# Two-layer decoder trunk on one core: the last head's searches, four tiles, one unit's gate and the summed blocks of stick-breaking attention are put elsewhere

## The chip, the cores and the metric

One core of a Trainium2 chip runs the whole kernel in one launch. The metric is the device time of an execution in microseconds. A core has TensorE (PE, matrix products into PSUM), VectorE (DVE), ScalarE (ACT), GpSimd (POOL, which here masks weights and issues the indirect row fetches) and SyncE (SP, which issues the other transfers). Each engine works through its own list of instructions in order, and they wait for one another by counting semaphores.

## The reference

512 tokens of 1024 float32 values pass two layers. A layer has a token mixer and a channel mixer, each behind an RMSNorm with shift and gain from a conditioning vector.

The token mixer has eight stick-breaking heads and four differential heads. For a stick-breaking head

```
log_fail = where(key < query, log_sigmoid(-z), 0)
after    = sum of log_fail over later keys
w        = where(key < query, exp(log_sigmoid(z) + after), 0);   y = w @ v
```

The channel mixer retrieves single-neuron experts. Each of eight heads scores a token against two sets of 128 keys, takes the best 16 of each (s, i), then the best 16 of the 256 sums, which name 16 of 16384 experts, with a softmax over their sums as gates g:

```
a = h . u[expert];  y = sum over 8 heads x 16 picks of  gelu(a) * g * v[expert]
```

## The kernel before

**Token mixer.** Four turns a layer, each with two stick-breaking heads (h = 0, 1) and one differential head. The keys are taken in four blocks of 128 from the last to the first: block p has kb = 3 - p, and its scores are kept for the queries from 128 kb on, 512 - 128 kb columns. `logits` makes z, ScalarE's `soften` the softplus, and VectorE (L1263, L1267) stores L = softplus, masked on the diagonal. `sums(p)` adds to z in PSUM the products NEG_UPPER @ L[kb] (L660) and NEG_ONES @ L[kk] for every later block kk (L663): none at p=0, 128 columns at p=1, 256 and 128 at p=2, and 384, 256 and 128 at p=3. Then ScalarE (`weigh`) exponentiates, GpSimd masks, and `values` multiplies with v. A float32 product is two instructions in the trace. Beside this VectorE makes the modulation of the next stage (L1207) and the rotary rope of dq (after block 2) and dk (after block 3).

**Channel mixer.** Tokens 0 to 255 (two chunks) take their experts by rows: 16 units (chunk x head), each 16 rows of u and 16 rows of v, 512 rows a layer, numbered in one sequence. GpSimd fetches row n with an indirect DMA (L1166) into a ring of eight as soon as row n - 8 is used; VectorE takes the product with a u row (L1417) or adds a v row (L1423). Ahead of a unit's v rows stand `gate_rows`, which needs ScalarE's exponential and gelu of that unit (`unit_gates`), and `topk` of the unit two further on, so at row 160 that of unit 6 and at row 192 that of unit 7.

Tokens 256 to 511 go densely, against all 16384 experts: 128 tiles of 128, in two halves of 64. TensorE transposes a tile of u (`turn_u`, L548, one tile ahead), ScalarE copies it out (L978), TensorE multiplies it with h (L558), and ScalarE applies gelu to a pair (L911). This starts beside the eight heads' queries (L525) and scores (L535): eight tiles stand behind each of heads 0 to 5, none behind head 6, and sixteen behind head 7. The query weights of a head are loaded by SyncE as soon as the scores before have read the buffer.

VectorE finds the dense tokens' picks meanwhile (`topk_dense`, one for each head and chunk, ending in L1379), ten rows between one search and the next. For each pair of heads ScalarE exponentiates (`gates_t`, L923) and VectorE divides (`gates_dense`, L1386 to L1390); that of the last pair stands on ScalarE ahead of tile 60 and signals `pre_done`. TensorE then transposes the picks (`turn_picks`), ScalarE copies them out (`picks_out`), and the map stage makes the gate of every expert for every dense token, in 32 batches of 8 tokens: VectorE's `columns` (L1432, L1437) and ScalarE's `p_batch` (L946, L950) make one-hot columns, TensorE multiplies them (L589), VectorE's `gate_batch` (L1448) multiplies the activations by the gates, and ScalarE's `keep_batch` (L962) keeps the second half's gates. VectorE takes one row after each batch, 164 to 195. In batch 16 ScalarE does `unit_gates(5)`.

Then come, on TensorE, the value tiles of the first half (L605), the activation tiles of the second half, and its value tiles. VectorE goes on with the rows from 196; with rows 368 and 432 start 32 kept gate products each (L1465), the first of which waits for the second half's activations. At the layer's end x is loaded back and both sums are added (L1504 to L1514).

The order on every engine is written out by hand; nothing plans it.

Of the kernel before, what the change touches and what calls it, by code (L numbers as in the profile page):

```python
# [66 lines left out]
G_BANK = [6, 4]  # L67
KEPT = 4
KEEP0 = 16 * 23
KEEP1 = 16 * 27  # L70
# [42 lines left out]
def build(nc, io, out):  # L113
    with ExitStack() as ctx:
# [93 lines left out]
        def small(*dims):  # L208
# [38 lines left out]
            "q_ev k_ev v_ev dqraw_ev dkraw_ev dv_mm dv_ev rope_mm dq_ready dk_ready "  # L247
            "z_done  ln_done L_done b_done w_exp w_masked pv_done ysb_ev "
            "s_done max_done p_exp dw_done wt_done wt_ev y_done y_sq yn_done yt_done yd_ev "
# [19 lines left out]
        def qcols(kb):  # L269
            return SEQ - P * kb  # L270
# [5 lines left out]
        def _(sp):  # L276
# [35 lines left out]
            with sp.Fori(0, DEPTH) as l:  # L312
# [114 lines left out]
                spill_x(CH - 1)  # L427
                for hd in range(HEADS - 2):
                    load_q(hd + 1)
                    more_u(8 * hd + 4, 8)  # L430
                load_q(HEADS - 1)
                more_u(HALF - 12, 12)
                all_v(0)
# [21 lines left out]
        def _(pe):  # L455
# [167 lines left out]
            def mix(i, last_turn):  # L623
# [31 lines left out]
                def sums(p):  # L655
                    kb = CH - 1 - p
                    for h in range(2):
                        bank = 2 + 2 * (p % 2) + h
                        pe.wait_ge(S["L_done"], 8 * i + 2 * p + h + 1)
                        last = pe.matmul(ps[:, bank, 0:qcols(kb)], C(NEG_UPPER), L[:, h, kb, 0:qcols(kb)],  # L660
                                         start=False, stop=(kb == CH - 1), skip_group_check=True)
                        for kk in range(kb + 1, CH):
                            last = pe.matmul(ps[:, bank, (kk - kb) * P:qcols(kb)], C(NEG_ONES),  # L663
                                             L[:, h, kk, 0:qcols(kk)], start=False, stop=(kk == CH - 1),
                                             skip_group_check=True)
                        last.then_inc(S["b_done"], 1)
# [99 lines left out]
            with pe.Fori(0, DEPTH) as l:  # L766
# [41 lines left out]
                for hd in range(HEADS):  # L808
                    query(l, hd, 0)
                    query(l, hd, 1)  # L810
                    head_scores(l, hd)
                    if hd == 0:
                        turn_u(l, 0, 0)
                    if hd < HEADS - 2:
                        act_tiles(l, 0, 8 * hd, 8 * hd + 8)
                act_tiles(l, 0, 8 * (HEADS - 2), HALF)
                turn_picks(l)
# [8 lines left out]
        def _(act):  # L826
# [160 lines left out]
            def channel_mix(l):  # L987

                for hd in range(HEADS):
                    stage_query(l, hd, 0)  # L990
                    stage_query(l, hd, 1)
                    stage_scores(l, hd)
                    if hd == 0:
                        u_out(l, 0, 0)
                    if hd % 2 == 0 and hd > 0:
                        gates_t(l, hd // 2 - 1)
                    if hd in (1, 2, 4, 5, 7):
                        unit_gates(l, (1, 2, 4, 5, 7).index(hd))
                    if hd < HEADS - 2:
                        for tile in range(8 * hd, 8 * hd + 8):  # L1000
                            act_tile(l, 0, tile)
                for tile in range(8 * (HEADS - 2), HALF):
                    if tile == HALF - 4:
                        gates_t(l, BLOCKS - 1)
                    act_tile(l, 0, tile)
                picks_out(l)
                for b in range(NB):
                    p_batch(l, b)
                    if b >= 1:
                        keep_batch(l, b - 1)  # L1010
                    if b == 16:
                        unit_gates(l, 5)
                keep_batch(l, NB - 1)
                for j in range(6, 9):
                    unit_gates(l, j)
# [164 lines left out]
        def _(dve):  # L1180
# [70 lines left out]
            def mix(i, t):  # L1251
# [6 lines left out]
                for p in range(CH):  # L1258
# [7 lines left out]
                    for h in range(2):  # L1266
                        dve.tensor_tensor(L[:, h, kb, 0:P], L[:, h, kb, 0:P], C(STRICT), ALU.mult).then_inc(S["L_done"], 1)  # L1267
                    dve.drain()
                    if p == 2:
                        rope(i, 0, dq_raw, dq, 0, "dq_ready")  # L1270
# [178 lines left out]

            def gate_maps(l, row0):  # L1450

                for b in range(NB):
                    columns(l, b)
                    if b >= 1:
                        gate_batch(l, b - 1)
                    rows(l, row0 + b, row0 + b + 1)
                gate_batch(l, NB - 1)
# [17 lines left out]
            def channel_mix(l):  # L1475

                dve.wait_ge(S["tr_done"], 4 * CH * l + 4 * CH)
                park()
                for hd in range(HEADS):
                    rows(l, 20 * hd, 20 * hd + 10)  # L1480
# [5 lines left out]
                    if hd % 2 == 0 and hd > 0:  # L1486
                        gates_dense(l, hd // 2 - 1)
                gates_dense(l, BLOCKS - 1).then_inc(S["pre_done"], 1)
                rows(l, 160, 164)
                dve.wait_ge(S["pq_ev"], ND * l + ND)  # L1490
                park()
                gate_maps(l, 164)
                rows(l, 196, KEEP0)
                kept_maps(l, 0, KEEP0)
# [164 lines left out]
```

## Time and profile before

| | us |
|---|---|
| median of 3 runs | 3883.69 (3882.17 to 3885.43) |
| profiled execution, its own time | 3883.39 |
| its span, first to last instruction | 3881.7 |
| TensorE busy | 3505.5 (90%) |
| VectorE busy | 2624.1 (68%) |
| GpSimd busy | 1382.6 (36%) |
| ScalarE busy | 981.8 (25%) |

All times in rows are microseconds from the span's start, if not marked ns. The chain that ended last is 61% TensorE and 24% VectorE; the rest is issue, transfers and ScalarE.

### The profile page before, as it was taken

What the parts mean: (1) busy time and instruction counts of PE and PEld (TensorE: products, weight loads), DVE (VectorE), ACT (ScalarE), POOL (GpSimd) and SP (SyncE); (2) the same over time, 40 slices, a digit from 0 to 9 for tenths busy, and PEclk for the clock granted to TensorE, in tenths of its full rate; (3) what the DMA queues carried; (4) which work ended last, traced back from release to release, by engine and by line L of the source; (5) the groups of instructions that cost most, each with busy time, mean ns of one, the idle gap of its engine ahead of it and who ended that gap; (6) DMA issues with size and microseconds to landing.
All of it is one profiled execution on the core that took longest, in us unless ns stands there. A gap on an engine that the chain in (4) does not pass through costs nothing.

```text
span 3881.7 us, 50533 instructions
## 1 busy us (share of the span) xinstructions
PE 3505.5 (90%) x13822; PEld 2245.4 (58%) x13822; DVE 2624.1 (68%) x5585; ACT 981.8 (25%) x2147; POOL 1382.6 (36%) x1220
## 2 busy tenths in 40 slices
PE   4998998999866999999978889989998579999997
PEld 2555444777654448884445554457767544688643
DVE  6555115899899777777555541279999987777774
ACT  1333102323254003330023330123223620133200
POOL 0000001445423665566500000034444245666663
PEclk9999999999988999999989999999998889999999
DMA  6321224788856999999952222168877579999997
GB/s 243 132 103 55 91 83 169 283 314 322 303 171 220 404 394 396 337 386 384 374 198 103 97 82 103 50 251 328 307 273 283 179 295 399 401 381 334 391 390 297
DMA packets 274015, 999.71 MB, mean 258 GB/s; under 512 B 31353, under 2 KB 48249, under 8 KB 262785
## 3 DMA queue, kind: packets, MB, share of 16 engines
q0 software_dynamic: 153600, 553.72, 37.7%
q1 hardware_dynamic: 120194, 443.42, 30.3%
q8 instruction: 92, 1.51, 0.2%
q14 instruction: 129, 1.06, 0.1%
HBM read 971.85 MB, written 25.17 MB: 257 GB/s over the span
## 4 chain that ended last, share of the span: by engine, by line
PE 61%; DVE 24%; issue 5%; DVEq 5%; DMA 3%; ACT 2%; ACTq 0%; POOL 0%; SPq 0%; POOLq 0%
PE ps L605 22%; PE ps L558 12%; PE ps L784 9%; DVE arena L1417 4%; DVE mod L1423 4%; PE ps L548 3%; DVE arena L1207 3%; PE ps L516 2%; DMA arena<-in_u_dram,idx 2%; PE ps L493 2%; PE ps L613 2%; PE ps L637 1%; DVE mod L1437 1%; DVEq L1425 1%; DVE arena L1313 1%
## 5 line engine op out<-in xcount | busy, mean ns | idle before, releaser
L1166 POOL DMA_INDIRECT arena<-in_u_dram,idx x512 | 647.5, 1265 | 1001.4 <-issue 648.4
L558 PE MATMUL ps<-hT,mod 128*128 128x256 f32 x4096 | 927.8, 380 | 0.0
L605 PE MATMUL ps<-arena 128*128 128x512 f32 x2048 | 881.6, 593 | 3.7 <-ACT hT L962 3.7
L1166 POOL DMA_INDIRECT arena<-in_v_dram,idx x512 | 638.8, 1248 | 621.8 <-DVE mod L1423 369.5
L558 PEld LDWEIGHTS ps<-hT,mod 128*128 128x128 f32 x4096 | 760.2, 191 | 93.3
L1417 DVE CUSTOM_DVE_ANT_0 arena<-arena 128x1024 f32<-128x1024 f32 x512 | 616.6, 1223 | 236.7 <-DMA arena<-in_u_dram,idx 233.1
L1423 DVE SCALAR_TENSOR_TENSOR mod<-arena,mod 128x1024 f32<-128x1024 f32 x512 | 657.1, 1283 | 122.7 <-DMA arena<-in_v_dram,idx 93.5
L605 PEld LDWEIGHTS ps<-arena 128*128 128x128 f32 x2048 | 389.6, 190 | 493.3 <-issue 493.2
L978 ACT COPY mod<-ps 128x512 f32<-128x512 f32 x512 | 274.6, 590 | 553.1 <-PE ps L548 553.1
L548 PE MATMUL ps<-const,arena 128*128 128x128 f32 x2048 | 269.0, 275 | 20.1 <-ACT mod L978 19.2
L548 PEld LDWEIGHTS ps<-const,arena 128*128 128x128 f32 x2048 | 239.1, 141 | 51.1 <-ACT mod L978 26.6
L525 PE MATMUL ps<-hT,arena 128*128 128x512 f32 x512 | 230.7, 610 | 14.0 <-DMA arena<-in_w_q_dram 11.7
L1207 DVE SCALAR_TENSOR_TENSOR arena<-arena,c_act 128x256 f32<-128x256 f32 x448 | 213.7, 484 | 40.9 <-DMA arena<-in_ada_w_dram 9.2
L1145 POOL TENSOR_SCALAR_AFFINE_SELECT arena<-arena 128x128 f32<-128x128 f32 x32 | 11.7, 378 | 615.8 <-ACT arena L1051 615.8
L784 PE MATMUL ps<-hT,arena 128*128 128x512 f32 x512 | 228.3, 605 | 2.7 <-ACT arena L1095 2.7
L1549 DVE TENSOR_TENSOR arena<-arena,ps 128x512 f32<-128x512 f32 x32 | 22.0, 688 | 306.6 <-PE ps L784 306.6
L525 PEld LDWEIGHTS ps<-hT,arena 128*128 128x128 f32 x512 | 99.9, 196 | 135.6 <-issue 135.0
L784 PEld LDWEIGHTS ps<-hT,arena 128*128 128x128 f32 x512 | 99.3, 194 | 128.2 <-issue 128.2
L911 ACT ACTIVATE arena<-ps 128x512 f32<-128x512 f32 x128 | 76.9, 601 | 371.6 <-PE ps L558 371.6
L589 PE MATMUL ps<-arena,mod 128*128 128x128 f32 x512 | 84.9, 334 | 76.9 <-issue 39.4
L589 PE MATMUL ps<-cos_sin,mod 128*128 128x128 f32 x512 | 86.5, 339 | 56.7 <-ACT mod L950 38.9
L516 PE MATMUL ps<-hT,arena 128*128 128x512 f32 x288 | 132.2, 614 | 3.2 <-ACT hT L860 1.9
(201 smaller groups left out, 3493.1 us busy)
## 6 DMA issues: line engine op xcount, KB each, us to landing
arena<-in_u_dram SPq DMA_DIRECT2D x256, 512.0 KB, 7.1
arena<-in_v_dram SPq DMA_DIRECT2D x256, 512.0 KB, 6.8
arena<-in_ada_w_dram SPq DMA_DIRECT2D x56, 1024.0 KB, 5.7
arena<-in_w_qkv_dram SPq DMA_DIRECT2D x48, 512.0 KB, 6.3
arena<-in_w_m_dram SPq DMA_DIRECT2D x16, 1536.0 KB, 6.8
arena<-in_w_q_dram SPq DMA_DIRECT2D x32, 576.0 KB, 6.5
gate_scratch<-hT SPq DMA_DIRECT2D x64, 256.0 KB, 2.2
hT<-gate_scratch POOLq DMA_DIRECT2D x128, 128.0 KB, 7.8
```

The source lines that it names most:

```text
L516: last = pe.matmul(ps[:, bank, :], w_qkv[:, g, k, :], hT[:, k, :], start=(k == 0), stop=(k == KD - 1))
L525: last = pe.matmul(ps[:, c, :], q_w[:, c, k, :], hT[:, k, :], start=(k == 0), stop=(k == KD - 1))
L548: last = pe.transpose(ps[:, 4 + h, k * P:(k + 1) * P], stream[:, slot, kk * P:(kk + 1) * P], C(IDENT))
L558: last = pe.matmul(ps[:, 6 + tile // 2 % 2, tile % 2 * NT:(tile % 2 + 1) * NT], u_turned[:, tile % 2, k * P:(k + 1) * P], hT[:, k, DT0:SEQ ...
L589: last = pe.matmul(ps[:, G_BANK[s] + t // 4, t % 4 * P:(t % 4 + 1) * P], p1[:, s, t * P:(t + 1) * P], q1[s][:, t * P:(t + 1) * P], start=T ...
L605: last = pe.matmul(ps[:, 2 * c + n, :], act_t[:, e, c * P:(c + 1) * P], stream[:, slot, n * 512:(n + 1) * 512], start=(half == 0 and e == ...
L784: last = pe.matmul(ps[:, 4 * s + b, :], w_m[:, s, k0 + k, :], rhs[:, k, :], start=(k == 0), stop=(k == n - 1))
L978: act.copy(u_turned[:, tile % 2, h * 512:(h + 1) * 512], ps[:, 4 + h, :]).then_inc(S["ut_ev"], 1)
L1166: pool.indirect_dma_start(out=ring[:, r % RING, :], out_offset=None, in_=table, in_offset=bass.IndirectOffsetOnAxis(ap=idx[:, j % 4, k:k + ...
L1207: last = dve.scalar_tensor_tensor(acc, ada_w[at % 3][:, k, :], c_act[:, k:k + 1], bias[:, cols] if k == 0 else acc, ALU.mult, ALU.add)
L1417: dve.tensor_tensor_reduce(row, row, h2[:, j % 2, :], 1.0, 0.0, ALU.mult, ALU.add, dots[:, j % 2, k:k + 1]).then_inc(S["row_used"], 1)
L1423: dve.scalar_tensor_tensor(total, row, coef[:, k:k + 1], total, ALU.mult, ALU.add).then_inc(S["row_used"], 1)
```

## The change

In the map stage and around it:

- Tiles 44 to 47 stand behind head 6's scores and no longer ahead of its query. SyncE's loads follow: head 7's query weights are issued ahead of tile 48's transfer.
- On VectorE head 7's two searches and the last `gates_dense` stand ahead of rows 140 to 159. Rows 140 to 160 stand between it and the maps; the maps take rows 161 to 191, and the last batch takes none.
- On ScalarE the last `gates_t` stands behind tile 63, ahead of `picks_out`, and `unit_gates(5)` behind the maps.
- In the sums VectorE adds, from p=2 on, the later block's L into the next one (a running total), and TensorE takes one NEG_ONES product for all later blocks. The new semaphore `T_done` orders it; VectorE's addition waits until the sums before have read what it overwrites.

```diff
+ENDS = [0, 8, 16, 24, 32, 40, 44, 48]
+G_ROW = 161
+G_END = 192
 # SyncE
-                for hd in range(HEADS - 2):
+                for hd in range(HEADS - 1):
                     load_q(hd + 1)
-                    more_u(8 * hd + 4, 8)
-                load_q(HEADS - 1)
-                more_u(HALF - 12, 12)
+                    first = STREAM + ENDS[hd]
+                    more_u(first, (STREAM + ENDS[hd + 1] if hd < HEADS - 2 else HALF) - first)
 # TensorE, sums(p)
-                        for kk in range(kb + 1, CH):
-                            last = pe.matmul(ps[:, bank, (kk - kb) * P:qcols(kb)], C(NEG_ONES),
-                                             L[:, h, kk, 0:qcols(kk)], start=False, stop=(kk == CH - 1),
-                                             skip_group_check=True)
+                        if p >= 2:
+                            pe.wait_ge(S["T_done"], 4 * i + 2 * p + h - 3)
+                        if p >= 1:
+                            last = pe.matmul(ps[:, bank, P:qcols(kb)], C(NEG_ONES), L[:, h, kb + 1, 0:qcols(kb + 1)],
+                                             start=False, stop=True, skip_group_check=True)
 # TensorE, heads
-                    if hd < HEADS - 2:
-                        act_tiles(l, 0, 8 * hd, 8 * hd + 8)
-                act_tiles(l, 0, 8 * (HEADS - 2), HALF)
+                    if hd < HEADS - 1:
+                        act_tiles(l, 0, ENDS[hd], ENDS[hd + 1])
+                act_tiles(l, 0, ENDS[-1], HALF)
 # ScalarE
-                for tile in range(8 * (HEADS - 2), HALF):
-                    if tile == HALF - 4:
-                        gates_t(l, BLOCKS - 1)
+                for tile in range(ENDS[-1], HALF):
                     act_tile(l, 0, tile)
+                gates_t(l, BLOCKS - 1)
                 picks_out(l)
                 for b in range(NB):
                     p_batch(l, b)
                     if b >= 1:
                         keep_batch(l, b - 1)
-                    if b == 16:
-                        unit_gates(l, 5)
                 keep_batch(l, NB - 1)
-                for j in range(6, 9):
+                for j in range(5, 9):
                     unit_gates(l, j)
 # VectorE, stick-breaking
+                    if p >= 2:
+                        for h in range(2):
+                            dve.wait_ge(S["b_done"], 8 * i + 2 * p + h - 1)
+                            dve.tensor_tensor(L[:, h, kb + 1, P:qcols(kb + 1)], L[:, h, kb + 1, P:qcols(kb + 1)],
+                                              L[:, h, kb + 2, 0:qcols(kb + 2)], ALU.add).then_inc(S["T_done"], 1)
 # VectorE, maps
-                    rows(l, row0 + b, row0 + b + 1)
+                    rows(l, G_ROW + b, min(G_ROW + b + 1, G_END))
 # VectorE, channel mixer
-                for hd in range(HEADS):
+                for hd in range(HEADS - 1):
...
+                topk_dense(l, HEADS - 1, 0)
+                topk_dense(l, HEADS - 1, 1)
                 gates_dense(l, BLOCKS - 1).then_inc(S["pre_done"], 1)
-                rows(l, 160, 164)
+                rows(l, 20 * (HEADS - 1), G_ROW)
                 dve.wait_ge(S["pq_ev"], ND * l + ND)
                 park()
-                gate_maps(l, 164)
-                rows(l, 196, KEEP0)
+                gate_maps(l)
+                rows(l, G_END, KEEP0)
```

## Rows read from the trace of the kernel before

**Rows 1.** Stretch by engine: PE, PEld, DVE, ACT, POOL busy, PEclk, DMA share, GB/s.
```profile
1232.00:1454.00 222.00, 221.59 (x526) 98.79 (x527) 162.34 (x266) 10.61 (x18) 138.82 (x108) 1.00 1.01 394
```

**Rows 2.** Chain that ended last, one turn: start, us, what.
```profile
196.20 0.22 PE ps L663 x2
...
202.00 0.65 PE ps L663 x4
...
208.23 1.30 PE ps L663 x6
```

**Rows 3.** Timeline of VectorE, same turn: start, busy, what [idle before].
```profile
203.79 0.49 DVE L1267 TENSOR_TENSOR arena<-arena,const 128x128 f32<-128x128 f32 x2
...
214.12 0.69 DVE L1273 COPY arena<-ps 128x512 f32 x1 [7.68 <-PE ps L675]
```

**Rows 4.** Timeline of TensorE, heads 6 and 7, both layers.
```profile
949.07 3.62 PE L558 MATMUL ps<-hT,mod 128*128 128x256 f32 x16
...
953.40 3.62 PE L558 MATMUL ps<-hT,mod 128*128 128x256 f32 x16
956.86 13.90 PE L525 MATMUL ps<-hT,arena 128*128 128x512 f32 x32
...
978.01 15.73 PE L525 MATMUL ps<-hT,arena 128*128 128x512 f32 x32 [5.42 <-DMA arena<-in_w_q_dram]
...
1062.14 1.97 PE L548 MATMUL ps<-const,arena 128*128 128x128 f32 x8 [10.29 <-ACT mod L978]
...
2864.90 13.90 PE L525 MATMUL ps<-hT,arena 128*128 128x512 f32 x32
...
2886.89 17.01 PE L525 MATMUL ps<-hT,arena 128*128 128x512 f32 x32 [6.26 <-DMA arena<-in_w_q_dram]
```

**Rows 5.** Map stage, layer 0, columns as in rows 1: batches 0-11, 28-30.
```profile
1079.48:1133.09 53.61, 32.51 (x187) 30.18 (x188) 51.06 (x95) 32.90 (x86) 15.80 (x12) 0.76 0.56 180
...
1202.40:1225.68 23.28, 7.81 (x43) 7.27 (x42) 21.47 (x60) 8.21 (x22) 4.28 (x3) 0.67 0.32 102
```

**Rows 6.** Timeline of VectorE: ends of searches (L1379), batch 0 (L1432), both layers.
```profile
962.96 0.23 DVE L1379 TENSOR_SCALAR arena<-arena 128x16 f32<-128x16 f32 x1
...
1061.08 0.23 DVE L1379 TENSOR_SCALAR arena<-arena 128x16 f32<-128x16 f32 x1
...
1079.48 1.23 DVE L1432 TENSOR_TENSOR cos_sin<-iota,h_row 128x1024 f32<-128x1024 f32 x1 [1.86 <-ACT h_row L935]
...
2870.18 0.23 DVE L1379 TENSOR_SCALAR arena<-arena 128x16 f32<-128x16 f32 x1
...
2985.09 1.23 DVE L1432 TENSOR_TENSOR cos_sin<-iota,h_row 128x1024 f32<-128x1024 f32 x1 [0.91 <-ACT h_row L935]
```

**Rows 7.** VectorE's busy time: rows 140-149, 150-159, row 160's gate and search.
```profile
1018.04:1030.53 12.49, 12.01 (x16) 1.00 0.80 279
1039.81:1052.32 12.51, 11.62 (x21) 1.00 0.94 336
1062.44:1072.21 9.77, 8.57 (x38) 0.77 0.31 87
```

**Rows 8.** Timeline of ScalarE: the last gates_t's table load.
```profile
1048.18 1.28 ACT L923 ACT_TABLE_LOAD   x1
```

**Rows 9.** Timeline of GpSimd: a fetch issued beside u rows, one beside a search.
```profile
1043.29 1.99 POOL L1166 DMA_INDIRECT arena<-in_u_dram,idx  x1 [0.30 <-issue]
...
1053.18 0.93 POOL L1166 DMA_INDIRECT arena<-in_v_dram,idx  x1 [0.30 <-issue]
```

**Rows 10.** Timeline of VectorE in the map stage, batch 18.
```profile
1162.88 0.69 DVE L1448 TENSOR_TENSOR arena<-arena,ps 128x512 f32<-128x512 f32 x1 [2.33 <-PE ps L589]
```

**Rows 11.** Waits of VectorE from 1576 to 1600, then its last row and reload.
```profile
DVE arena L1465 <- ACT arena L911: 11.9, 1, 11.9
...
1927.03 1.28 DVE L1423 SCALAR_TENSOR_TENSOR mod<-arena,mod 128x1024 f32<-128x1024 f32 x1 [0.30 <-DMA arena<-in_v_dram,idx]
...
1950.39 2.36 DVE L1504 TENSOR_TENSOR mod<-mod 128x1024 f32<-128x1024 f32 x2 [22.08 <-DMA x_res<-x_scratch]
```

More of the change, by code:

```diff
@@ L247, in build @@
             "q_ev k_ev v_ev dqraw_ev dkraw_ev dv_mm dv_ev rope_mm dq_ready dk_ready "
-            "z_done  ln_done L_done b_done w_exp w_masked pv_done ysb_ev "
+            "z_done  ln_done L_done T_done b_done w_exp w_masked pv_done ysb_ev "
             "s_done max_done p_exp dw_done wt_done wt_ev y_done y_sq yn_done yt_done yd_ev "
@@ L998, in channel_mix @@
                         unit_gates(l, (1, 2, 4, 5, 7).index(hd))
-                    if hd < HEADS - 2:
-                        for tile in range(8 * hd, 8 * hd + 8):
+                    if hd < HEADS - 1:
+                        for tile in range(ENDS[hd], ENDS[hd + 1]):
                             act_tile(l, 0, tile)
-                for tile in range(8 * (HEADS - 2), HALF):
-                    if tile == HALF - 4:
-                        gates_t(l, BLOCKS - 1)
+                for tile in range(ENDS[-1], HALF):
                     act_tile(l, 0, tile)
+                gates_t(l, BLOCKS - 1)
                 picks_out(l)
@@ L1448, in gate_batch, with gate_maps @@
                 dve.tensor_tensor(acts, acts, gate.rearrange("p t i -> p i t"), ALU.mult).then_inc(S["gm_done"], 1)
-            def gate_maps(l, row0):
+            def gate_maps(l):
                 for b in range(NB):
```

## The prediction

> **What bounds the kernel now.** I read the page's busy table and the chain of waits first. In each layer the chain runs through TensorE from the first value stage to the layer's end: with the search heads and maps over, TensorE is busy 221.59 of 222 us [rows 1]. Whatever comes before the value stage therefore moves the end one for one, and VectorE's row work behind it is hidden. Before the value stage I read the timelines of each engine in two places.
>
> In a mixing turn the chain stays on TensorE through the sums, NEG_ONES products included [rows 2]; VectorE idles 7.68 us shortly after [rows 3]. In the channel stage two engines take turns. TensorE streams tiles of 4.33 us, stops 5.42 us (layer 0) and 6.26 us (layer 1) for head 7's query weights, and 10.29 us before tile 62's transposes, because ScalarE is held on head 7's searches [rows 4]. VectorE is busy up to the maps, then the maps run at VectorE's pace: TensorE is busy 32.51 of 53.61 us there, VectorE 51.06 [rows 5]. So what decides is when VectorE starts batch 0 (1079.48 and 2985.09, [rows 6]), and how long 32 batches take.
>
> **The sums.** A head's sums lose 128 of their columns at block p=2 and 384 at p=3. The chain shows 0.22 us for one pass of 128 columns, 0.65 for 256+128, 1.30 for 384+256+128 [rows 2]. So 256 columns are 0.43 and 384 are 0.65. Block p=2 falls from 0.65 to 0.43, p=3 from 1.30 to 0.65, each twice (two heads): 2 x 0.22 + 2 x 0.65 = 1.74 us a turn, 8 turns, **13.9 us**.
> The four new additions (128 and 256 columns, twice each) have no row of before. From both sides: nothing, and the 0.24 us of one 128-column product with STRICT in [rows 3] doubled for 256 columns, 0.5 each; I take 1.5 us of VectorE a turn. Those of p=3 start about 204.35, and are done about 205.2; TensorE reaches sums(3) about 206.9, so its new wait costs nothing. Behind it in VectorE's queue stands rope of dk, which would end about 207.2, while its reader starts after the last values, about 211. The p=2 additions wait for sums(1), which end at 197.1, 4 us before their reader. The additions' cover is the 7.68 us idle; without it they would cost 12 us in all.
>
> **Tiles between heads 6 and 7.** Tiles 44 to 47 move behind head 6's scores, so head 7's weights (issued when those scores end) land during 17.3 us of tiles, and SyncE issues them ahead of tile 48, whose transfer is needed only three tiles later. The 5.42 us go. What is late next: ScalarE reaches head 6's gates_t(2) 17.3 us sooner, and it needs head 5's last search, over at 962.96 + 0.15 [rows 6]. Layer 0: tile 43 ends 956.86 - 17.3 = 939.5; query and scores take 15.7 (956.86 to 978.01 - 5.42), 955.2; transposing 45 and multiplying 44 takes 4.33, 959.6. In the stall that the trace has, TensorE resumed 1.06 us after the search's last instruction (1061.08, 1062.14): here 964.0. Three tiles 13.0, plus 1.4 for the slower matmuls that follow a stop, 978.4 (a query took 13.9 us without one, 15.73 after 5.42 us and 17.01 after 6.26 [rows 4], so 1.8 and 3.1 more; these stops are 4.4 and 3.6 us, and I take less); head 7 15.6, 994.0; 16 tiles less one transpose, 68.4: **1062.4**. Layer 1 the same way from 2864.90 and 2870.18 [rows 4, 6]: 2847.6, 2863.3, 2867.6, resume 2871.2, 2885.6, 2901.2, **2969.6**. Only 1.4 and 4.4 us of the gain are left.
>
> **Searches ahead of rows.** This is the decisive step. VectorE has head 7's scores at hand at 1018.04, does both searches (9.28 us each, the gap between the first two stretches of [rows 7]; the other took 8.9) and is done about 1036.2. Next in its queue is gates_dense(3), which waits for the exponential. ScalarE now makes that after tile 63's gelu, so after TensorE's last tile. The table load of before begins at 1048.18 [rows 8], 0.7 us after tile 59's multiply (1062.14 - 10.29 - 4.33 = 1047.5), and takes 1.28; from the exponential to VectorE's next gate it is 1.1 (1062.44 less 1061.08 + 0.27): **3.2 us after the last tile**. VectorE idles from 1036.2 to about 1065, some 29 us, and the 20 rows that used to fill that time stand behind the wait and in front of the maps. They are 140 to 159; then row 160 with its gate and search of unit 6.
> Rows 140 to 159 took 12.49 + 12.51 = 25.0 us [rows 7], 23.6 of it busy. Now they come in one run without a search in it. Eight are in the ring. POOL takes 1.99 + 0.30 us to issue a fetch beside u rows, and 0.93 + 0.30 beside a search [rows 9]. Low end 23.6; high end, eight rows at the measured 1.25 are 10.0, and twelve at 2.29 make 37.5. The four v rows and the waits let POOL get ahead, and the tile transfers have stopped (DMA share 0.31 against 0.94, [rows 7]); nearest is the measured 25.0, I take 26.5.
> The Trainium skill, "SBUF — State Buffer", section "SBUF: two separate sides", says that VectorE and GpSimd hold a shared port pair for a whole instruction, a VectorE operation with two SBUF inputs included if GpSimd's reads SBUF, and that descriptors for GpSimd's transfers starve meanwhile. It speaks against taking the searches out of the run of rows, and 1.99 against 0.93 agrees. By that rule for every fetch the total is 3916.5, by the measured run of rows 3894.5.
> Gate and search 9.77 [rows 7], row 160 with its pause 1.5. Start of maps, layer 0: 1062.4 + 3.2 + 26.5 + 9.8 + 1.5 = 1103.4, **+23.9**; layer 1: 2969.6 + 41.0 = 3010.6, **+25.5**.
>
> **The maps.** Both versions carry 31 rows that count (the 32nd of before is hidden by the last batch's own chain), so no row is saved. Unit 7's gate and search go: batches 28 to 30 took 23.28 us, three batches with v rows are 3 x 4.5 = 13.5 (twelve took 53.61), **-9.8**. Unit 5's exponential and gelu in ScalarE held VectorE 2.33 us [rows 10]: **-2.3**. With rounding 12.2 a layer. The work moves behind the maps: unit 5's two table loads and activations (some 3.3 us, which VectorE waits for at row 192), the search of 9.8, four rows more at up to 2.29. VectorE is up to 22 us later then. Cover: it waits 11.9 us for tiles at the first kept batch anyway, and stops at 1928 while the layer's end waits for x until 1950.39 [rows 11]. I cost it at nothing; what the 11.9 us don't take, 10 us, ends in the second gap.
>
> **Sum.** Layers: 23.9 - 12.2 and 25.5 - 12.2 are +25.0. Turns -13.9. Together **+11.1**. The profiled execution took 3883.39 us (span 3881.7), 0.3 below the median of the runs: 3894.5.
>
> **Rivals.**
> 1. *TensorE doesn't stop before tile 46* (the other side). If head 5's search is over by then, TensorE runs through: last tiles end at 1056.4 and 2964.5, 11.1 us less for both layers, and the total is 3883.4; with the rows at 23.6 too, 3877.6. It decides from the point at which VectorE finishes that search before 959.6 and 2867.6. Against it: the search is at 963.1 and 2870.3 and nothing ahead of it changes. Chance 0.15.
> 2. *The sums save nothing*: the additions come after TensorE is there. They would have to be 1.7 us later than worked out. For it: they wait for the sums before. 3894.5 + 13.9 = 3908.4. Chance 0.06.
> 3. *The run of rows is bound by fetches*: 37.5 in place of 26.5, so 22 more, 3916.5; half of it, 3905. For: [rows 9]. Against: POOL gains time in every pause. Chance 0.12.
> 4. *VectorE is late at the layer's end*, by rows that collide with x's reload: if the first cover fails, VectorE ends at 1950 and the last three fetches of 2.29 lie beside the reload: 7 us a layer, 3908. Chance 0.07.
> 5. *The searches do what they are meant to*, the exponential being ready at 1036: maps would start at 1036.2 + 1.1 + 37.8 = 1075.1, 4.4 earlier than before; two layers of -4.4 - 12.2 and the turns give 3836. ScalarE's order excludes it. Chance 0.02.
> My forecast has 0.58.
>
> **How the numbers follow.** Forecast 3894.5, of its own 3889 to 3901. To hold 8 in 10 the range takes in rival 1 with tie, and half of rivals 2 and 3: 3884 to 3907. What a measurement tells from no change is 0.2%, 7.8 us, so slower begins at 3891.5. Slower: four fifths of the forecast's chance, and rivals 2 to 4, 0.71. Same: the rest of the forecast and two thirds of rival 1, 0.21. Faster: a third of rival 1, rival 5, and a remainder, 0.08.
>
> **What the changed profile would show.** VectorE idle some 29 us a layer before the reduction of gates_dense(3), ended by ScalarE; batch 0 at +24 and +25 us against the heads' start; then 140.5 us to the first value matmul; no wait for w_q before head 7, but one of about 4 us for ScalarE before tile 46's transposes; NEG_ONES passes of 0.43 and 0.65 with no idle before them. I am wrong if the idle in front of gates_dense(3) is under 20 us, if rows 140 to 159 take under 22 or over 33 us, or if turns shorten by other than 1.7 us.

## The result, and the profile after

The changed kernel took 3901.1 us (median of 9 runs, 3894.4 to 3912.7) against 3883.7 us for the kernel before (9 runs): a ratio of 1.0043, 95% interval 1.0031 to 1.0055. It is slower by some 17 us, where 11 were predicted. The profiled execution took 3900.51 us (span 3898.8), 17.1 above that of before, and the table below is made from these two executions. Its landmarks are the first query matmul of the channel stage ("heads"), the columns of batch 0 ("batch 0") and the first value matmul ("values"); all of them are read from the timelines.

| stretch, us | before | after | difference | predicted |
|---|---|---|---|---|
| start to heads, layer 0 | 650.56 | 640.66 | -9.9 | -7.0 |
| heads to batch 0 | 428.9 | 459.7 | +30.8 | +23.9 |
| batch 0 to values | 152.7 | 142.3 | -10.4 | -12.2 |
| values to heads of layer 1 | 1326.4 | 1319.6 | -6.8 | -7.0 |
| heads to batch 0 | 426.5 | 454.6 | +28.1 | +25.5 |
| batch 0 to values | 153.5 | 140.6 | -12.9 | -12.2 |
| values to end | 743.1 | 741.3 | -1.8 | 0 |
| sum | | | +17.1 | +11.1 |

The sums, in TensorE's timeline after (start, busy, line, output and input, count). Each line, one float32 product in two instructions, is one head's:

```profile
120.19 0.60 PE L667 MATMUL ps<-arena,const 128*128 128x256 f32 x2
121.27 0.59 PE L667 MATMUL ps<-arena,const 128*128 128x256 f32 x2
...
125.99 0.81 PE L667 MATMUL ps<-arena,const 128*128 128x384 f32 x2
127.49 0.81 PE L667 MATMUL ps<-arena,const 128*128 128x384 f32 x2
```

No row has idle time ahead of it, and there are two instructions a head where the kernel before had four and six ([rows 2]). VectorE's additions, in its timeline, with the row that had waited 7.68 us in [rows 3]:

```profile
195.48 0.29 DVE L1272 TENSOR_TENSOR arena<-arena 128x128 f32<-128x128 f32 x1 [0.21 <-PE ps L667]
196.13 0.33 DVE L1272 TENSOR_TENSOR arena<-arena 128x128 f32<-128x128 f32 x1 [0.36 <-PE ps L667]
...
203.41 0.76 DVE L1272 TENSOR_TENSOR arena<-arena 128x256 f32<-128x256 f32 x2
...
211.38 0.69 DVE L1278 COPY arena<-ps 128x512 f32 x1 [5.24 <-PE ps L678]
```

The additions are 1.4 us a turn (0.29 + 0.33 + 0.76) and come out of an idle time that is still 5.24 us long.

Heads 6 and 7 on TensorE after, answering to [rows 4]:

```profile
930.93 13.90 PE L527 MATMUL ps<-hT,arena 128*128 128x512 f32 x32
...
954.74 1.97 PE L550 MATMUL ps<-const,arena 128*128 128x128 f32 x8 [3.75 <-ACT mod L981]
...
970.63 13.90 PE L527 MATMUL ps<-hT,arena 128*128 128x512 f32 x32
...
2874.31 1.15 PE L550 MATMUL ps<-const,arena 128*128 128x128 f32 x8 [1.62 <-ACT mod L981]
```

The wait for head 7's weights is gone, and a new stop for ScalarE stands ahead of tile 46's transposes. VectorE from head 7's last search to batch 0, both layers, answering to [rows 6]:

```profile
1028.94 0.23 DVE L1384 TENSOR_SCALAR arena<-arena 128x16 f32<-128x16 f32 x1
1057.49 0.22 DVE L1391 TENSOR_REDUCE arena<-arena 128x4 f32<-128x64 f32 x1 [28.31 <-ACT arena L926]
...
1058.18 5.41 DVE L1428 SCALAR_TENSOR_TENSOR mod<-arena,mod 128x1024 f32<-128x1024 f32 x4
...
1079.20 1.23 DVE L1422 CUSTOM_DVE_ANT_0 arena<-arena 128x1024 f32<-128x1024 f32 x1 [1.16 <-DMA arena<-in_u_dram,idx]
...
1088.58 0.16 DVE L1403 RECIPROCAL arena<-arena 128x1 f32<-128x1 f32 x1 [0.21 <-issue]
...
1100.38 1.23 DVE L1437 TENSOR_TENSOR cos_sin<-iota,h_row 128x1024 f32<-128x1024 f32 x1 [0.39 <-issue]
...
2974.27 0.22 DVE L1391 TENSOR_REDUCE arena<-arena 128x4 f32<-128x64 f32 x1 [27.54 <-ACT arena L926]
2974.96 5.41 DVE L1428 SCALAR_TENSOR_TENSOR mod<-arena,mod 128x1024 f32<-128x1024 f32 x4
...
3016.96 1.23 DVE L1437 TENSOR_TENSOR cos_sin<-iota,h_row 128x1024 f32<-128x1024 f32 x1 [0.39 <-issue]
```

Here is the loss. VectorE has done its searches at 1029, stands still for 28.3 us until ScalarE's exponential, and only then takes up 20 rows that depend on nothing it has waited for. They take 30.2 us (1058.18 to 1088.37) and 30.0 us, with TensorE all but idle (0.87 and 1.54 us busy). The same stretch in windows (span, then busy PE, PEld, DVE, ACT, POOL, PEclk, DMA share, GB/s):

```profile
1058.18:1088.37 30.19, 0.87 (x6) 0.64 (x6) 24.17 (x37) 5.60 (x16) 23.21 (x17) 0.52 0.72 242
2974.96:3004.96 30.00, 1.54 (x6) 1.14 (x6) 24.16 (x37) 5.69 (x16) 23.02 (x17) 0.50 0.75 245
```

VectorE is busy 24.2 of 30 us there; 5.5 and 5.3 us of the rest are waits of u rows for their fetches. GpSimd's timeline of that stretch, answering to [rows 9], shows issues of both lengths:

```profile
1064.70 1.12 POOL L1166 DMA_INDIRECT arena<-in_u_dram,idx  x1 [0.30 <-issue]
1066.13 1.98 POOL L1166 DMA_INDIRECT arena<-in_u_dram,idx  x1 [0.30 <-issue]
1068.42 1.99 POOL L1166 DMA_INDIRECT arena<-in_u_dram,idx  x1 [0.30 <-issue]
...
1080.39 0.94 POOL L1166 DMA_INDIRECT arena<-in_u_dram,idx  x1 [0.30 <-issue]
```

What was moved behind the maps is paid out of VectorE's waits. Its wait at the first kept batch, 11.9 us in [rows 11], in the waits of VectorE (total, times, longest):

```profile
DVE arena L1470 <- issue: 0.4, 1, 0.4
```

Its waits for x's reload were 22.08 us in [rows 11] and 20.5 at the end of layer 1 before. After, in its timeline:

```profile
1962.82 2.36 DVE L1511 TENSOR_TENSOR mod<-mod 128x1024 f32<-128x1024 f32 x2 [15.28 <-DMA x_res<-x_scratch]
...
3874.54 2.36 DVE L1511 TENSOR_TENSOR mod<-mod 128x1024 f32<-128x1024 f32 x2 [10.67 <-DMA x_res<-x_scratch]
```

So 11.5 + 6.8 us of lateness in layer 0 are absorbed, and more than 10 us of cover are left.

### The profile page after: what moved, and what is told of

Read it like the earlier page. It is cut to its first block, busy times and chain, and to the rows that moved or that the text cites. A ratio compares the mean times of both kernels' runs of the same rounds, so it can differ in the third digit from the quotient of the medians.

```text
span 3898.8 us, 50373 instructions
## 1 busy us (share of the span) xinstructions
PE 3485.2 (89%) x13726; PEld 2230.1 (57%) x13726; DVE 2636.8 (68%) x5617; ACT 981.7 (25%) x2147; POOL 1390.5 (36%) x1220
## 3 DMA queue, kind: packets, MB, share of 16 engines
q14 instruction: 129, 1.06, 0.1%
## 4 chain that ended last, share of the span: by engine, by line
PE 69%; DVE 18%; issue 5%; DVEq 3%; ACT 2%; DMA 2%; ACTq 0%; POOL 0%; SPq 0%; POOLq 0%
PE ps L607 22%; PE ps L560 17%; PE ps L787 9%; PE ps L550 4%; PE ps L527 3%; DVE arena L1422 3%; DVE arena L1207 3%; DVE mod L1428 3%; PE ps L518 2%; PE ps L495 2%; DVE mod L1442 2%; PE ps L615 2%; PE ps L639 1%; PE ps L662 1%; DMA arena<-in_u_dram,idx 1%
## 5 line engine op out<-in xcount | busy, mean ns | idle before, releaser
L1166 POOL DMA_INDIRECT arena<-in_u_dram,idx x512 | 662.9, 1295 | 1068.9 <-issue 652.7
L591 PEld LDWEIGHTS ps<-cos_sin,mod 128*128 128x128 f32 x512 | 79.4, 245 | 145.2 <-issue 95.4
```

The costliest lines, as they stand in the source:

```text
L591: last = pe.matmul(ps[:, G_BANK[s] + t // 4, t % 4 * P:(t % 4 + 1) * P], p1[:, s, t * P:(t + 1) * P], q1[s][:, t * P:(t + 1) * P], start=T ...
L1166: pool.indirect_dma_start(out=ring[:, r % RING, :], out_offset=None, in_=table, in_offset=bass.IndirectOffsetOnAxis(ap=idx[:, j % 4, k:k + ...
```

## The experiments

They were made in three comparisons, each on another chip with its own runs of the kernel before: medians of 3916.9, 3883.0 and 3902.5 us. On the first and the third the runs of one kernel scatter by 50 us and more, so ratios there have wide intervals, and the stretches of the profiled executions carry the verdict: heads to batch 0 is 426 to 429 us in both layers of the kernel before, and 454 to 460 in three profiles of the changed kernel. The largest scatter lies elsewhere, in the stretch from the first value matmul to the heads of layer 1: 1316 to 1327 us in nine profiles, but 1338 to 1355 in the four of the first comparison and 1354 in experiment 10. Its cause stays open.

**1. The sums alone, on the kernel before.**

The sums and the additions are edited as in the change; a part of it:

```diff
 # TensorE, sums(p)
...
+                        if p >= 2:
+                            pe.wait_ge(S["T_done"], 4 * i + 2 * p + h - 3)
+                        if p >= 1:
+                            last = pe.matmul(..., C(NEG_ONES), L[:, h, kb + 1, 0:qcols(kb + 1)], ...)
...
```

> The kernel before with the summed blocks alone. My theory: what a turn saves is the products that go, 2 x 0.22 + 2 x 0.65 = 1.74 us by the rows of before and 1.75 by the traces of both kernels over the sums alone, and the four additions cost nothing; 8 turns, 14 us: 3870. Rival A: the 17 us by which the turns of the changed kernel are shorter in its trace all belong to this edit, in every run: 3867. Rival B: the additions reach TensorE late and nothing is left: 3884.

Ratio 0.9968 (0.9935 to 1.0), or 12 us faster, with 14 expected; the interval reaches no difference. Heads start at 640.77 us, as in the changed kernel, and at 649.90 in experiment 2 on the same chip; heads to batch 0 is 426.4 and 429.7, as before. The gain before the heads of layer 0 is thus the sums' and theirs alone.

**2. The tiles alone, on the kernel before.**

The order of TensorE, with `ENDS` and SyncE's loads as in the change:

```diff
...
-                    if hd < HEADS - 2:
-                        act_tiles(l, 0, 8 * hd, 8 * hd + 8)
+                    if hd < HEADS - 1:
+                        act_tiles(l, 0, ENDS[hd], ENDS[hd + 1])
...
```

> The kernel before with tiles 44 to 47 between heads 6 and 7 alone. My theory: the wait for head 7's weights (5.42 and 6.26 us) goes, a wait of 2 to 5 us for ScalarE comes in front of tile 46, and what is left moves TensorE towards tile 62, where it waits for VectorE's searches anyway; the end does not move: 3883 to 3885. Rival A: the two waits come off the end: 3872. Rival B: ScalarE's wait costs more than it gives: 3888 or more.

Ratio 0.9982 (0.9953 to 1.0011): no difference that can be told. Heads to batch 0 is 425.7 and 428.3 us against 428.9 and 426.5. TensorE's timeline shows why:

```profile
974.39 13.90 PE L525 MATMUL ps<-hT,arena 128*128 128x512 f32 x32
...
1058.55 1.97 PE L548 MATMUL ps<-const,arena 128*128 128x128 f32 x8 [10.63 <-ACT mod L978]
```

Head 7's query has no wait any more, and the stop ahead of tile 62 is no shorter than in [rows 4]: 10.63 us for 10.29 in layer 0, and 11.09 for 6.69 in layer 1. VectorE sets this stretch and TensorE's 5 us only move. The stop of 2 to 5 us that was expected ahead of tile 46 didn't come in this profile: 0.24 us in layer 0 and none in layer 1.

**3. Rows 140 to 159 ahead of the wait.** The changed kernel with

```diff
+                rows(l, 20 * (HEADS - 1), 20 * HEADS)
                 gates_dense(l, BLOCKS - 1).then_inc(S["pre_done"], 1)
-                rows(l, 20 * (HEADS - 1), G_ROW)
+                rows(l, 20 * HEADS, G_ROW)
```

> The changed kernel with rows 140 to 159 ahead of the last gates_dense, so that VectorE has work while it would wait for the exponential; nothing else differs. My theory: the changed kernel is slow because VectorE idles 28.31 and 27.54 us there with these rows still to do. Then the rows (25 to 30 us) run from 1029 to about 1059, the exponential is ready at 1057, and batch 0 starts near 1072 in place of 1100, in layer 1 near 2990 in place of 3017: about 55 us less, 3846, clearly under the kernel before. Rival A: beside the tiles' transfers a run of u rows is bound by fetches at 2.05 us each (the pace behind the maps), 38 us for the 20 rows: 39 less, 3862. Rival B: the order of rows against the wait does not matter, since something else holds the maps: 3901.

Ratio 0.9882 (0.9836 to 0.9928): 46 us faster than before, 39 by the medians, the fastest run 3848. VectorE's timeline:

```profile
1026.45 5.40 DVE L1428 SCALAR_TENSOR_TENSOR mod<-arena,mod 128x1024 f32<-128x1024 f32 x4
...
1059.95 0.22 DVE L1391 TENSOR_REDUCE arena<-arena 128x4 f32<-128x64 f32 x1 [2.64 <-ACT arena L926]
...
1072.42 1.22 DVE L1437 TENSOR_TENSOR cos_sin<-iota,h_row 128x1024 f32<-128x1024 f32 x1 [0.38 <-issue]
...
2998.04 1.23 DVE L1437 TENSOR_TENSOR cos_sin<-iota,h_row 128x1024 f32<-128x1024 f32 x1 [0.39 <-issue]
```

The wait of 28.31 us has become 2.64 us in layer 0, and there is none in layer 1; rows 140 to 159 took 31 us. Heads to batch 0 is 431.6 and 428.8 us, 28 and 26 less than the changed kernel, which had lost 31 and 28: the order of these rows against the wait is nearly the whole loss. The profiled execution itself took 3905.8 us, the slowest run of this kernel, because values to the heads of layer 1 took 1355 us in it.

**4. The last exponential ahead of tile 60,** rows left behind the wait.

```diff
                 for tile in range(ENDS[-1], HALF):
+                    if tile == HALF - 4:
+                        gates_t(l, BLOCKS - 1)
                     act_tile(l, 0, tile)
-                gates_t(l, BLOCKS - 1)
```

> The changed kernel with the last exponential ahead of tile 60 on ScalarE, as the kernel before has it, and the searches still ahead of the rows. My theory: the searches are over at 1029 and tile 60 comes at about 1038, so VectorE idles about 11 us and not 28; batch 0 starts some 17.5 us earlier in each layer: 3901 - 35 = 3866. TensorE does not stop at tile 62, since the searches are over by then. Rival A: TensorE stops there all the same, 10 us a layer, but VectorE holds the maps: still 3866, with the stop seen. Rival B: the exponential's place is not the cause: 3901.

Ratio 0.9934 (0.9903 to 0.9965), 26 us faster than before (19 by the medians), with 18 expected. The wait is shorter and doesn't end before ScalarE has come to tile 60:

```profile
1043.11 0.22 DVE L1392 TENSOR_REDUCE arena<-arena 128x4 f32<-128x64 f32 x1 [13.06 <-ACT arena L926]
...
1083.58 1.23 DVE L1438 TENSOR_TENSOR cos_sin<-iota,h_row 128x1024 f32<-128x1024 f32 x1 [0.39 <-issue]
```

Heads to batch 0 is 441.7 and 440.1 us, 18.0 and 14.5 below the changed kernel. Either half of the edit pays: an earlier end of the wait, or the work ahead of it.

**5. The changed kernel again,** on the second chip and on the third.

> The changed kernel again, to have it and the kernel before on the same chip as the three below. Both theories: the difference to the kernel before is that of the first comparison, 1.0043, or some 17 us slower; its stretches are those of its first profile: 460 and 455 us from the first head's queries to the first batch of columns, and rows 140 to 159 in 30.2 and 30.0 us.

> The changed kernel once more, for the three below on the same chip. Both theories: 1.003 to 1.0045 of the kernel before.

Ratios 1.0039 (1.0025 to 1.0053) and 1.0016 (0.9988 to 1.0044). The second interval takes in no difference at all, so the times on the third chip show none; the stretches do. Heads to batch 0: 456.0 and 455.1, then 460.0 and 454.5 us. The loss in this stretch is not one chip's. Rows 140 to 159 took 28.7 and 30.5 us, then 29.3 and 27.3: their time scatters by 3 us between executions of the same kernel.

**6. Unit 6's search among the rows.**

```diff
-                rows(l, 20 * (HEADS - 1), G_ROW)
+                rows(l, 140, 150)
+                topk(l, 6)
+                rows(l, 150, G_ROW)
```

> Only the place of unit 6's search is moved, from behind row 160 to between rows 149 and 150. Theory (the fetches bound the run of rows: GpSimd takes 1.99 + 0.30 us to issue each while VectorE computes u rows at 1.15 us each, and 1.24 us beside a search): during the 9.6 us search some seven fetches are issued with nothing used, so rows 150 to 159 find their data: the rows of 140 to 159 take 25 to 26 us without the search instead of 30, and the first batch of columns stands some 4.5 us earlier in each layer (455 and 450 us behind the first head's queries), 9 us less in all than the changed kernel. Rival (the rows wait on something that the search doesn't relieve, such as the time of a landing from its issue or slots that come free late): still 30 us, and no change of the time.

The edit also keeps `topk` from running a second time at row 160. 3888.17 us, ratio 1.0011 (0.9998 to 1.0023), 8.3 us below the changed kernel on the same chip: 9 were expected. GpSimd's timeline as the search begins:

```profile
1072.56 1.99 POOL L1166 DMA_INDIRECT arena<-in_u_dram,idx  x1 [0.30 <-issue]
1074.85 0.94 POOL L1166 DMA_INDIRECT arena<-in_u_dram,idx  x1 [0.30 <-issue]
```

VectorE's timeline, the last gate's reduction and batch 0:

```profile
1061.63 0.22 DVE L1391 TENSOR_REDUCE arena<-arena 128x4 f32<-128x64 f32 x1 [29.48 <-ACT arena L926]
...
1098.44 1.23 DVE L1437 TENSOR_TENSOR cos_sin<-iota,h_row 128x1024 f32<-128x1024 f32 x1 [0.39 <-issue]
```

The issue falls from 1.99 to 0.94 us, and no row waits for a fetch. Rows 140 to 159 take 24.0 us in both layers without the search (25 to 26 expected), against 28.7 and 30.5 in the control of experiment 5 on this chip. From the last gate's reduction to batch 0 it is 36.8 us in both layers against 41.4 and 43.2: 5 and 6 us less for the same instructions. The fetches did bind the run of rows. But batch 0 stands at 457.3 and 454.9 us behind the heads, where 455 and 450 were expected and the control has 456.0 and 455.1: in this one profile the reduction came about as much later (420.5 and 418.1 us behind the heads' start, 414.6 and 411.9 in the control) as the rows took less. The gain in time rests on the medians; experiment 9 is on the late reduction.

**7. A drain behind each u row of 144 to 159.**

```diff
                         if k == TOPK - 1:
                             dve.drain().then_inc(S["dots_done"], 1)
+                        elif 144 <= n < 160:
+                            dve.drain()
```

> VectorE empties its pipeline behind each u row of 144 to 159, as it does behind each v row of the value stage, where GpSimd's issue took 1.07 us instead of 1.99. Theory (back-to-back u rows hold GpSimd's issue up): the issue beside these rows falls from 1.99 to about 1.1 us, the waits on fetches go, and although each row costs some 0.1 to 0.2 us more, rows 140 to 159 take about 27.5 us instead of 30: 2.5 us less in each layer, 5 in all. Rival (the fetch takes 1.99 us whatever VectorE does between rows): the issue stays near 2 us, the run stays at 30 us, and the drains are hidden in the waits: no change.

GpSimd's timeline:

```profile
1064.14 1.06 POOL L1166 DMA_INDIRECT arena<-in_u_dram,idx  x1 [0.30 <-issue]
1065.51 1.06 POOL L1166 DMA_INDIRECT arena<-in_u_dram,idx  x1 [0.30 <-issue]
```

The issues beside these rows take 1.06 to 1.13 us, none of them 1.99; the rows come every 1.37 us instead of 1.15, none waits, and rows 140 to 159 take 27.4 us in both layers: what was expected. In the total it doesn't show: 3897.84 us, ratio 1.0033 (1.0022 to 1.0044) against 1.0039 (1.0025 to 1.0053). A gain of 5 us is neither shown nor excluded by these intervals; in the profile there are 1.7 and 3.5 us of it from the reduction to batch 0 (39.7 us twice, against 41.4 and 43.2 in the control), and they are more than offset by a later reduction (418.2 us behind the heads' start, twice). So back-to-back u rows double the time of GpSimd's issue, and a short pause between them is enough to end that.

**8. Rows and exponential together.**

```diff
+                rows(l, 20 * (HEADS - 1), 20 * HEADS)
                 gates_dense(l, BLOCKS - 1).then_inc(S["pre_done"], 1)
...
+                    if tile == HALF - 4:
+                        gates_t(l, BLOCKS - 1)
...
```

> Rows 140 to 159 stand ahead of the last gate's wait, and ScalarE makes that gate's exponential ahead of tile 60: both earlier edits in one. In the run with the rows moved alone VectorE still waited 2.64 us for the exponential behind row 159 (1057.31 to 1059.95) and 31 us passed for rows 140 to 159. Theory (what bounds the way to the maps is then the run of rows alone): 1.5 to 2.6 us per layer less than with the rows moved alone, so the first batch of columns 429 and 426 us behind the first head's queries and, against the changed kernel, some 60 us less in all (28 + 26 from the rows, 2 to 5 from the exponential). Rival (the last four tiles, which then wait for ScalarE's 2.6 us of table loads, set the time at which the maps can begin): no gain over the rows alone, some 54 us less than the changed kernel.

3842.64 us, ratio 0.9885 (0.987 to 0.99): 53.8 us below the changed kernel on that chip and 40.4 below before. VectorE passes the last gate without a wait, in its timeline:

```profile
1058.27 0.22 DVE L1392 TENSOR_REDUCE arena<-arena 128x4 f32<-128x64 f32 x1 [0.25 <-issue]
```

TensorE idles ahead of the picks:

```profile
1059.10 1.54 PE L578 MATMUL ps<-const,g_row 128*128 128x128 f32 x6 [4.82 <-DVE g_row L1396]
```

Heads to batch 0 is 432.2 and 432.4 us, no less than with the rows alone, on another chip. The rival has it, by its number, though not by its reason: TensorE had 4.8 us to spare. The rows didn't take up the 2.64 us of wait: 140 to 159 took 30.5 and 29.7 us here, against 31 in experiment 3. VectorE came to row 140 later, 389.0 and 390.0 us behind the heads' start against 385.6 and 384.9. So these two profiles don't tell what the earlier exponential is worth beside the moved rows.

**9. The exponential of heads 4 and 5 behind tile 46.**

```diff
-                    if hd % 2 == 0 and hd > 0:
+                    if hd in (2, 4):
                         gates_t(l, hd // 2 - 1)
...
                             act_tile(l, 0, tile)
+                            if tile == 46:
+                                gates_t(l, 2)
```

> Only ScalarE's exponential of heads 4 and 5 is moved, from behind head 6's scores to behind tile 46. In five profiles of kernels with the changed head order TensorE stopped ahead of tile 46's transposes for 3.8 to 7.3 us in layer 0 and 1.6 to 6.3 us in layer 1, as long as head 5's last search on VectorE was late; and the transposes and multiply behind a stop took 1.97 + 5.63 us instead of 1.04 + 3.62. Theory (each microsecond of this stop delays the last tile, the last exponential and the maps one for one): the stop is gone, the wait of VectorE ahead of the last gates_dense ends 6 to 10 us sooner in layer 0 and 4 to 9 us in layer 1, and the time is 10 to 19 us below the changed kernel, about that of the kernel before. Rival (the exponential's two table loads, 2.6 us, or the head's next step hold TensorE as long in another place): no change.

TensorE's timeline, tile 44's multiply and tile 46's transposes:

```profile
946.29 3.62 PE L560 MATMUL ps<-hT,mod 128*128 128x256 f32 x16
950.13 1.46 PE L550 MATMUL ps<-const,arena 128*128 128x128 f32 x8 [0.22 <-issue]
```

The stop is gone: 0.22 us in place of 5.92 us in the control's layer 0, and none of 2.38 in its layer 1. The last gate's reduction stands 410.8 and 412.6 us behind the heads' start, against 418.0 and 414.5 in the control: 7.2 us, as expected, and 1.9, less than the 4 expected. The times (ratio 1.0004, 0.9979 to 1.0028, against 1.0016, 0.9988 to 1.0044) agree with any gain from none to 15 us. In layer 0 the stop was 3.75, 3.94 and 5.92 us in the profiles of the changed kernel, 0.32, 1.95, 7.25, 7.12 and 7.09 in those of experiments 3, 4, 6, 7 and 8, and 2.12 in that of 10. Experiments 3, 4 and 6 to 8 don't touch what stands ahead of it in layer 0, so this is scatter between chips and executions, and a part of what set the reduction late in the profiles of 6 to 8. The traces show its two sides. In the profiles of 6, 7 and 8 head 5's last search on VectorE ends 315 to 317 us behind the heads' start, against 312 to 313 in 3 and in the first two profiles of the changed kernel; and in 3 and 4 TensorE comes to head 6's query late, at 293.0 and 293.7 against 289 to 291 elsewhere. Why either is late stays open.

**10. The changed kernel with the old sums.**

> The changed kernel with one NEG_ONES product per later block again and without the running total. Theory (the sums gave exactly the columns that they lose): 1.75 us more in each of eight turns, 14 us more than the changed kernel. Rival A (with them goes a better clock in the stretches between, 3 us in the first comparison): 17 us more. Rival B (the additions cost VectorE time that TensorE waits for elsewhere): less than 8 us more.

Ratio 1.0081 (1.0049 to 1.0114) against 1.0016: some 25 us more, between 8 and 42 by the two intervals taken together, where 14 were expected. That the sums pay is shown, the size isn't settled by this: the profiled executions are 45 us apart, and 28 us of that lie in the stretch from values to the heads of layer 1, the one that scatters (1354 us against 1326). Heads start at 650.26 us here; they start at 650.56 and 649.90 in the two other profiles with the old sums, and in eleven profiles with the new ones between 635.41 and 641.84.

**11. All of it:** 8 with the drains of 7 and the edit of 9.

> The changed kernel with rows 140 to 159 ahead of the last gate's wait, that gate's exponential ahead of tile 60, VectorE's pipeline emptied behind u rows 144 to 159, and the exponential of heads 4 and 5 behind tile 46. The first two together gave 0.9885 of the kernel before, with rows 140 to 159 in 30.7 us, VectorE at them without a pause, and TensorE idle 4.8 us between tile 63 and the picks. Theory (this run of rows is the path): with the drains it takes 27.4 us, as in the run with drains alone, 3.3 us less in each layer; the tiles' stop has 4.8 us of slack and gives nothing: 6 to 7 us less than 0.9885, or 0.9868. Rival (the last tiles are the path as well): with the stop gone too, nothing else changes; if the drains only wait out what the fetches would, 0.9885 stays.

Ratio 0.9901 (0.9868 to 0.9934) on the third chip: not told apart from 8. Its profiled execution, the fastest run, took 3837.3 us, with 430.5 and 425.2 us from heads to batch 0, 1.7 and 7.2 less than in 8. Rows 140 to 159 took 29.8 and 28.2 us, not 27.4: they run beside the tile transfers now, and some rows wait up to 0.95 us all the same. The expected 6 to 7 us below 8 are thus neither shown nor excluded. Experiments 3, 4, 8 and 11 beat the kernel before by intervals clear of 1; 8 is the best with a tight interval, though from four runs.

## Why the prediction was right, point by point

- **What bounds.** Right: the stretches add up to the measured 17.1 us, with nothing taken back behind batch 0. In experiment 8 as well: values to the heads of layer 1 took 1317.1 us, 1317.8 in its control. In 3 and 4 this stretch took 1355 and 1338 us, within the scatter of that chip, so they don't test it.
- **The sums, -13.9.** The mechanism held: products of 256 and 384 columns, no wait on TensorE, additions free. The time in front of the heads of layer 0 fell by 9.9 and not by 7.0, and by 8 to 15 us over all the profiles. Inside a turn the sums' rows give the 1.75 us. More than half of the remaining 2.9 us lies between them in the third turn, in a group of matmuls that follows an idle time of 1.9 us in both kernels: it took 4.15 us before (305.22 to 309.37) and 2.51 after (300.20 to 302.71). Four products of 512 columns in it (`L713` before, `L716` after) took 1.88 us before and 1.13 after. The windows around them, of before and then of after (columns as above), show the granted clock at 0.58, near the lower level of 1.2 GHz, and at 1.00, which is 2.4 GHz:

```profile
307.50:309.40 1.90, 1.90 (x6) 0.54 (x5) 0.00 (x0) 0.87 (x4) 0.00 (x0) 0.58 0.00 0
```

```profile
301.60:302.80 1.20, 1.20 (x7) 0.40 (x5) 0.00 (x0) 0.86 (x4) 0.00 (x0) 1.00 0.00 0
```

Why it was granted in one and not in the other was not tested. With the value stages around them the turns came out at -18.5, 4.6 better than predicted. That layer 1's part, -6.8, meets the 7.0 is luck in some measure: the stretch that holds it took 1317.8 us in the second profile of the changed kernel and 1326.5 in the third.
- **Tiles between heads 6 and 7.** The wait for weights went, and the stop ahead of tile 46 came as predicted, by the mechanism predicted (ScalarE behind head 5's last search): 3.75 and 1.62 us, with 4.4 and 3.6 predicted. The last gate's reduction stood at 416.8 and 411.9 us against 415.0 and 414.2 predicted. Its scatter between executions (411.9 to 420.5) had no place in the working. Rival 1, no stop at all, did not occur in this profile, but it needs no edit: with the same order of heads and tiles the stop was 0.24 and 0.32 us in layer 0 of experiments 2 and 3 and absent in layer 1. The working treated as fixed what scatters, and a chance of 0.15 was low for it. Experiment 9 made it, and it gave 9 us in the two layers of a profile, where 11.1 were worked out.
- **Searches ahead of rows.** The decisive step held: idle 28.31 and 27.54 us (29 predicted), the gate's reduction 2.4 us behind the last tile's products (3.2 predicted), the rows behind it.
- **The mis-sized term: the run of rows.** 26.5 us were taken, 30.2 and 30.0 measured: +7.2 us for both layers together (27.3 to 30.5 in the two controls). I had chosen the value near the run that has a search in it and allowed GpSimd to get ahead in the pauses. Early in the run there are none: with a search put in, the stretch fell by 5 and 6 us (experiment 6), with a drain behind each u row by 2 and 3 (experiment 7). Rival 3 was thus a third right: it is the fetches. What kept it from 37.5 is seen in GpSimd's timeline: the 37.5 priced twelve issues at 1.99 us, and the first four take 1.07 to 1.36, and those beside rows that wait fall to as little as 0.94.
- **The skill's rule.** The Trainium skill, "SBUF — State Buffer", section "SBUF: two separate sides", has VectorE hold a port pair shared with GpSimd for a whole instruction. The trace agrees in kind: 1.99 us beside back-to-back u rows, 1.06 with drains between, 0.94 beside a search. That it is this port isn't shown by any run, and what the section says of descriptors that can't be written is said of VectorE's two-port modes; for a tensor_tensor with both inputs in SBUF it infers that they are not held up. The price that it gives, some 620 ns that become 3100, is that of a transfer beside a VectorE copy; the price beside u rows was what was needed.
- **Gate, search and row 160.** 12.0 us for 11.3, and 0.7 for the last gate's own three instructions, which the sum had left out: 1.4 a layer.
- **The maps.** 142.3 and 140.6 us for 140.5 predicted.
- **What was moved behind the maps.** Free in the profile, as costed: the wait at the first kept batch fell from 11.9 to 0.4 us, the second gap from 22.08 to 15.28.
- The errors sum up: +9.5 in front of the maps (rows 7.2, gates and search 2.8, the tile stop -0.5), +1.1 in the maps, -4.6 in the turns and the value stages, together +6.0: 17.1 for 11.1. The total is nearer than its parts: without the 4.6 us that came off by themselves it would have been 10.6 us over.

## What to carry to other kernels

When an instruction that waits is moved forward in an in-order queue, ask what stands behind it that doesn't need what it waits for: here 20 rows, 30 us a layer, put behind a wait that ended 28 us after the searches were done. A run of work that lives on fetches must be priced at the fetch's issue rate beside that very work, not at the rate of the old place, where other work had let the fetches get ahead. And a wait taken from an engine that isn't the bound (the tiles alone) buys nothing until the other engine has been moved.

## What was not expected of the hardware

GpSimd's issue of an indirect fetch goes back from 1.99 to 1.06 us when VectorE merely drains its pipeline between two operations, at 0.22 us a row. And shortening a few matmuls by 7 us brought 9.9 in the pair of profiles; 1.6 us of the surplus came from a stretch that ran at a granted clock of 1.00 instead of 0.58. What decides that stays open, and so does the rest.
